# Two scatter accumulators and full 128-row indirect DMAs in a mixture-of-experts kernel

## The reference

```python
def moe_ffn(x, router_w, router_bias, w_gate, w_up, w_down, sw_gate, sw_up, sw_down):
    ...
    _, idx = lax.top_k(scores + router_bias.astype(jnp.float32), TOP_K)
    ...
    padded = (counts + MOE_ROWS - 1) // MOE_ROWS * MOE_ROWS
    ...
    def expert_block(args):
        tok, e = args
        xb = xt[tok]
        h = jax.nn.silu(xb @ w_gate[e]) * (xb @ w_up[e])
        return h @ w_down[e]

    y = lax.map(expert_block, (row_tok.reshape(n_blocks, MOE_ROWS), blk_exp))
    y = y.reshape(P, D) * row_gate[:, None].astype(x.dtype)
    routed = jax.ops.segment_sum(y, row_tok, num_segments=T)
    shared = (jax.nn.silu(xt @ sw_gate) * (xt @ sw_up)) @ sw_down
    return (routed + shared).reshape(B, S, D)
```

## Time and profile before

| | us |
|---|---|
| median of 3 runs | 2637.62 (2608.13 to 2641.2) |
| the profiled execution | 2625.82 |
| its span, first to last instruction | 2623.9 |

### The profile page before, as it was taken

How to read it: one execution, slowest core, us unless ns; L and a number is a source line. 1 busy time by engine, 2 the same in 40 slices (tenths; PEclk the granted TensorE clock), 3 DMA queues, 4 the chain that set the end, 5 groups by cost and what they waited for, 6 DMA issues and landing times.

```text
span 2623.9 us, 35527 instructions
## 1 busy us (share of the span) xinstructions
PE 2323.8 (89%) x9437; PEld 1630.5 (62%) x9437; DVE 1695.1 (65%) x1753; ACT 1070.3 (41%) x1199; POOL 783.7 (30%) x682
## 2 busy tenths in 40 slices
PE   7652997899999999869999999798999999999995
PEld 4220455666666666647988888554666666666663
DVE  5998455666666667553257788545666666666665
ACT  2334014455555555422233333202455555555552
POOL 3663022444434434320000000002334443444432
PEclk9885989999999999988999999899999999999997
DMA  6110137999999999943232222232899999999995
GB/s 205 42 54 0 35 126 240 334 341 362 356 356 333 332 342 352 318 152 112 89 89 65 81 80 71 85 109 86 284 340 354 358 343 337 327 357 340 337 348 163
DMA packets 189297, 592.57 MB, mean 226 GB/s; under 512 B 18781, under 2 KB 88453, under 8 KB 153908
## 3 DMA queue, kind: packets, MB, share of 16 engines
q1 hardware_dynamic: 165140, 517.92, 54.1%
q0 software_dynamic: 24096, 73.88, 12.0%
HBM read 547.11 MB, written 51.38 MB: 228 GB/s over the span
## 4 chain that ended last, share of the span: by engine, by line
PE 35%; DMA 27%; DVE 12%; POOLq 11%; issue 9%; POOL 4%; ACT 1%; SPq 0%; DVEq 0%; ACTq 0%
DMA acc<-BIG,IDXS 22%; PE PS L1455 10%; POOLq L546 9%; DVE BIG L1084 6%; PE PS L1439 5%; PE PS L1237 4%; DMA BIG<-xrows,IDXG 3%; PE PS L1367 3%; PE PS L1346 3%; PE PS L1271 2%; POOL IDXS L586 2%; DMA W<-in_exp_w_up 2%; POOL IDXG L572 1%; PE PS L1468 1%; PE PS L1493 1%
## 5 line engine op out<-in xcount | busy, mean ns | idle before, releaser
L995 DVE TENSOR_TENSOR WL<-W,WH 128x2048 fp32r<-128x2048 f32 x276 | 627.9, 2291 | 276.6 <-ACT WH L691 276.0
L691 ACT ACTIVATE WH<-W 128x2048 fp32r<-128x2048 f32 x276 | 523.0, 1911 | 127.0 <-DMA W<-in_exp_w_up 118.0
L1367 PE MATMUL PS<-W,BIG 128*128 128x512 f32 x1104 | 510.6, 606 | 2.0 <-DVE BIG L1007 2.0
L1346 PE MATMUL PS<-WH,XH 128*128 128x512 f32 x1104 | 443.5, 402 | 5.8 <-DVE XL L988 5.5
L1346 PE MATMUL PS<-WH,XL 128*128 128x512 f32 x1104 | 432.2, 391 | 0.0
L1346 PE MATMUL PS<-WL,XH 128*128 128x512 f32 x1104 | 430.3, 390 | 0.0
L595 POOL DMA_INDIRECT acc<-BIG,IDXS x138 | 304.1, 2204 | 313.4 <-issue 295.3
L1367 PEld LDWEIGHTS PS<-W,BIG 128*128 128x128 f32 x1104 | 205.1, 196 | 209.3 <-issue 206.7
L1346 PEld LDWEIGHTS PS<-WH,XH 128*128 128x128 f32 x1104 | 208.1, 189 | 48.4 <-issue 8.7
L1346 PEld LDWEIGHTS PS<-WH,XL 128*128 128x128 f32 x1104 | 207.5, 188 | 45.2
L1346 PEld LDWEIGHTS PS<-WL,XH 128*128 128x128 f32 x1104 | 208.3, 189 | 39.2
(11 more groups left out here) (233 smaller groups left out, 3174.4 us busy)
## 6 DMA issues: line engine op xcount, KB each, us to landing
W<-in_exp_w_gate SPq DMA_DIRECT2D x138, 1024.0 KB, 8.1
W<-in_exp_w_up SPq DMA_DIRECT2D x138, 1024.0 KB, 11.3
W<-in_exp_w_down SPq DMA_DIRECT2D x138, 1024.0 KB, 7.0
RAW<-in_w_kv SPq DMA_DIRECT2D x48, 512.0 KB, 3.8
RAW<-in_attn_w_q SPq DMA_DIRECT2D x24, 512.0 KB, 3.7
W<-in_conv_w_in SPq DMA_DIRECT2D x8, 1024.0 KB, 11.4
acc<-BIG SPq DMA_DIRECT2D x9, 512.0 KB, 3.7
W<-in_conv_w_out SPq DMA_DIRECT2D x4, 1024.0 KB, 6.6
```

The costliest lines, as they stand in the source:

```text
L691: A(WH[:, s, c, :], W[:, 3 * s + c, :], ACT.Copy).then_inc(s_wh[l], 1)
L995: v.tensor_tensor(WL[s][:, c, :], W[:, 3 * s + c, :], WH[:, s, c, :].bitcast(F32), ALU.subtract).then_inc(s_wl[l], 1)
L1346: last = mm(PS[:, 3 + s, :].rearrange("p (a b) -> p a b", a=2), a, w, start=(k == 0 and i == 0), stop=(k == KT - 1 and i == 2))
L1367: last = mm(PS[:, 5 + h, :], HTm[:, s, k * P:(k + 1) * P], wd[:, k, h * 512:(h + 1) * 512], start=(k == 0), stop=(k == 1))
```

## The change

- `acc` loses its 128 spare rows, and each layer gets a second table of 512 rows, `acc_odd[l]`, which is set to zero at the start from a cleared tile (2 MB each).
- Blocks with an even number scatter to `acc`, those with an odd one to `acc_odd[l]`. `scatter(b)` waits for scatter `b - 2` alone; each slot has a semaphore of its own. `out_low` and `out_high` wait for the same event as before, named by the new semaphores.
- `some_slots` and `by_size` are gone. Each gather and scatter names all 128 rows, with a bounds check of T - 1 in both.
- After the loop SyncE loads both tables, 8 transfers of 512 KB instead of 4, and VectorE adds the two tiles ahead of the statistics (4 additions a layer).
- The semaphores of the routing tables (`s_pj`, `s_tb`) are one for both layers.

```diff
-                def some_slots(b):
-
-                    return [pool.value_load(IDX[i:i + 1, bass.ds(b, 1)].bitcast(I32), min_val=0, max_val=T + P)
-                            for i in (48, 64, 80, 96)]
-
-                def by_size(slots, rows):
...
                 def gather(b, s):
 
-                    slots = some_slots(b)
                     pool.tensor_copy(IDXG[:, s:s + 1], IDX[:, bass.ds(b, 1)]).then_inc(s_ic[l], 1)
                     pool.wait_ge(s_ic[l], b + 1 if isinstance(b, int) and b < 3 else b * 2 - 2)
                     pool.sem_inc(s_go, 1)
...
-                    by_size(slots, rows)
...
+                    pool.indirect_dma_start(XG[:, s, :], None, xrows, bass.IndirectOffsetOnAxis(IDXG[:, s:s + 1], axis=0),
+                                            bounds_check=T - 1, oob_is_err=False).then_inc(s_ga[l][s], 16)
+
+                def scatter(b, s, it, copies):
+
+                    if not (isinstance(b, int) and b < 2):
+                        pool.wait_ge(s_scat[l][s], it * 16)
+                        pool.sem_inc(s_go, 1)
                     pool.tensor_copy(IDXS[:, s:s + 1], IDX[:, bass.ds(b, 1)]).then_inc(s_ic[l], 1)
                     pool.wait_ge(s_ic[l], copies)
                     pool.wait_ge(s_ya[l], b + 1)
                     pool.wait_ge(s_yv[l], b + 1)
-                    if not (isinstance(b, int) and b == 0):
-                        pool.wait_ge(s_scat[l], b * 16)
                     pool.sem_inc(s_go, 1)
...
+                    pool.indirect_dma_start((acc, acc_odd[l])[s], bass.IndirectOffsetOnAxis(IDXS[:, s:s + 1], axis=0),
+                                            YB[:, s, :], None, bounds_check=T - 1, oob_is_err=False,
+                                            compute_op=ALU.add).then_inc(s_scat[l][s], 16)
...
+                sp.wait_ge(s_scat[l][0], n * 16)
+                sp.wait_ge(s_scat[l][1], n * 16)
                 for t in range(NT):
-                    if t == 0:
-                        sp.wait_ge(s_scat[l], n * 32)
                     sp.dma_start(X[:, t, :], acc[t * P:(t + 1) * P, :]).then_inc(s_xin[t], 16)
+                    sp.dma_start(XO[:, t, :], acc_odd[l][t * P:(t + 1) * P, :]).then_inc(s_xin[t], 16)
...
-            sp.dma_start(acc[T:T + P, :], XG[:, 0, :]).then_inc(s_zero, 16)
+            for l in range(2):
+                sp.dma_start(acc_odd[l].rearrange("(n p) d -> p n d", p=P),
+                             XG[:, 0:1, :].broadcast_to([P, NT, D])).then_inc(s_zero, 16)
...
-                        dve.wait_ge(s_xin[n], 16 * (r // 2 + 2))
+                        dve.wait_ge(s_xin[n], 16 + 32 * (r // 2 + 1))
+                        link(v.tensor_tensor(X[:, n, :], X[:, n, :], XO[:, n, :], ALU.add))
```

More of the change, by code:

```diff
@@ L47, in build @@
     xrows = nc.dram_tensor("xrows", [T, D], F32, kind="Internal").ap()
-    acc = nc.dram_tensor("acc", [T + P, D], F32, kind="Internal").ap()
+    acc = nc.dram_tensor("acc", [T, D], F32, kind="Internal").ap()
+    acc_odd = [nc.dram_tensor(f"acc_odd{i}", [T, D], F32, kind="Internal").ap() for i in range(2)]
     etab = nc.dram_tensor("etab", [2, OVER], I32, kind="Internal").ap()
@@ L181, in build @@
         XG = big(13568, 2, D)
+        XO = big(13568, NT, D)
         YB = big(17664, 2, D)
@@ L216, in build @@
         s_ob = sem("overflow_bases")
-        s_pj = [sem(f"onehots{i}") for i in range(2)]
-        s_tb = [sem(f"table_steps{i}") for i in range(2)]
+        s_pj = sem("onehots")
+        s_tb = sem("table_steps")
         s_tab = sem("tables_ready")
@@ L245, in build @@
         s_yv = [sem(f"expert_out_high_copied{i}") for i in range(2)]
-        s_scat = [sem(f"scattered{i}") for i in range(2)]
+        s_scat = [[sem(f"scattered{i}_{k}") for k in range(2)] for i in range(2)]
         s_ph, s_pl = sem("piece_high"), sem("piece_low")
@@ L574, in gather @@
                     pool.sem_inc(s_go, 1)
-                    def rows(r):
-                        pool.indirect_dma_start(XG[0:r, s, :], None, xrows,
-                                                bass.IndirectOffsetOnAxis(IDXG[0:r, s:s + 1], axis=0),
-                                                bounds_check=T - 1, oob_is_err=False).then_inc(s_ga[l][s], 16)
-                    by_size(slots, rows)
-                def scatter(b, s, copies):
-                    slots = some_slots(b)
+                    pool.indirect_dma_start(XG[:, s, :], None, xrows, bass.IndirectOffsetOnAxis(IDXG[:, s:s + 1], axis=0),
[4 more added lines that the diff above has]
+                        pool.sem_inc(s_go, 1)
                     pool.tensor_copy(IDXS[:, s:s + 1], IDX[:, bass.ds(b, 1)]).then_inc(s_ic[l], 1)
@@ L605, in moe, with step @@
                     pool.wait_ge(s_acc[l][k], 16 * NT // 2)
-                def step(b, s):
+                def step(b, s, it):
                     pool.wait_ge(s_tx[l], b + 2)
                     gather(b + 3, 1 - s)
-                    scatter(b, s, b * 2 + 5)
-                step(0, 0)
-                step(1, 1)
+                    scatter(b, s, it, b * 2 + 5)
+                step(0, 0, 0)
+                step(1, 1, 0)
                 with pool.Fori(1, n - 2) as it:
-                    step(it * 2, 0)
-                    step(it * 2 + 1, 1)
-                step(n * 2 - 4, 0)
-                for k in range(3):
-                    scatter(n * 2 - 3 + k, (1 + k) % 2, n * 4 - 2 + k)
+                    step(it * 2, 0, it)
+                    step(it * 2 + 1, 1, it)
+                step(n * 2 - 4, 0, n - 2)
+                scatter(n * 2 - 3, 1, n - 2, n * 4 - 2)
+                scatter(n * 2 - 2, 0, n - 1, n * 4 - 1)
+                scatter(n * 2 - 1, 1, n - 1, n * 4)
             def mix_in(l, n):
@@ L1319, in moe @@
                                   start=(n == 0 and j == 0), stop=(n == NT - 1 and j == 7))
-                    last.then_inc(s_tb[l], 1)
+                    last.then_inc(s_tb, 1)
                 sh_down(2)
```

63 lines of the change are left out of this document (21 added, 42 removed).

## The result

| | before | after |
|---|---|---|
| median | 2632.92 us (2608.13 to 2641.2) | 2706.14 us (2704.09 to 2707.84) |
| span of the profiled execution | 2623.9 us | 2704.8 us |
| loops, first to last output copy, layer 0 and 1 | 718 and 732 us | 752 and 772 us |

The ratio is 1.0285, with a 95% interval of 1.0235 to 1.0336: slower, by 73 us of median and 81 us of span. 74 of these 81 us lie in the two loops; the rest is at their ends. The forecast was 2795 us, so the sign was right and the size about half.

A forecast was written before the change was run, and what follows sets the result against it. The prediction took the DMA engines to be within a few per cent of the bound, with TensorE close. It summed 2625.8 + 156 (loops) + 10 (additions) = 2792 us, put the median at 2795, range 2660 to 2890 us.

The forecast's parts named there:

- What bounds the kernel now: Expert block loops: DMA engines within a few per cent of the bound; late gathers stretch TensorE's 10.0 us to 10.8.
- Part 1: Second accumulator and removed branches: gathers start earlier, worth at most 0.8 us a block, nothing where DMA becomes slower.
- Part 2: 128 named rows in gathers and scatters: real rows load half the engines, 12.0 us a block for 10.8.
- Rows, 4.2 us: Most loaded DMA engine, each block: 8 gathered and 8 scattered rows at 0.27 us each, over 1.02.
- Weights, 8.15 us: DMA engines' time for a block's weights, even over all 16: 8.3 us, over 1.02.
- The lower bound: Block pace with quickest rows: weights 7.65 us at 411 GB/s plus 16 rows at 0.24 us, over 1.02: 11.2 us.
- Steps counted: Loops of both layers: 130 of 138 blocks take the slower pace, 130 x (12.0 - 10.8) = +156 us.
- Part 3: Ends of the layers: four added VectorE tiles a layer, +10 us; reads about +1 us a layer; zero stores at most 2.
- Hidden anyway: Rival for the loops: row at 0.2 us, weights 7.65, pace 10.7 to 11.0 us, 2623 to 2662 us; chance 0.12.
- Spread evenly: Rival on row placement: engines share rows evenly, pace 10.0 to 10.2 us, 2532 to 2558 us; chance 0.13.
- TensorE's clock: Rival for the loops: steady waits lower the clock, TensorE's 10 us grow to 13 or more, 2948 us; chance 0.10.
- What would show it: Signs in the profile after: copies 11.2 to 12.4 us apart, TensorE 80 to 88% busy, DMA some 80%, up-matrix waits doubled.

The follow-up runs named there:

- before_early: Kernel before with only GpSimd's order changed, gather b + 4 issued ahead of scatter b: 2597.6 us, ratio 0.9857, 10.59 us a block.
- one_acc_plain: Kernel after with one accumulator and the old wait for scatter b - 1, 128 rows named in plain order: 2694.6 us, ratio 1.0236.
- the four placements: Kernel after and three copies with only the slots of rows permuted; 4.2, 6.4, 7.1, 7.8 rows on the busiest engine: 10.19, 10.95, 11.41, 11.79 us a block.
- plain_5mb: Kernel after with one of three gate and up terms, gate and up matrices loaded twice, no low parts: 3320.3 us, 16.05 us a block.
- norows_5mb: plain_5mb with every row index out of bounds, so all rows are named and none moved: 2877.1 us, 12.65 us a block.
- norows_short_early: norows_short_pe with gather b + 4 issued ahead of scatter b: 2299.2 us, ratio 0.8738, 8.25 us a block.
- two_acc_spread: Kernel after with the rows of a block dealt out over all 16 DMA engines by permuted slots: 2554.0 us, ratio 0.9701.
- plain_short_pe: Kernel after with one of the three terms of the gate and up products: 2690.3 us, ratio 1.0215, 11.38 us a block.
- the packed kernel: Kernel after with slots permuted so that one DMA engine is filled with eight rows before the next: 2755.3 us, ratio 1.0467.
- norows_short_pe: plain_short_pe with every row index out of bounds, so all rows are named and none moved: 2518.0 us, ratio 0.9555, 10.05 us a block.

## Why the prediction was right in kind and wrong in size

The direction and the mechanism were right: slower, because the rows of a block sit on half of the engines. The size was not: +1.2 us a block was forecast and +0.60 measured, +162 us in all against +73. The stated range of 2660 to 2890 us holds the measured 2706 because it is wide, not because the sum was right.

- **What bounds the kernel now** held. DMA was within a few per cent of being the bound: a DMA share of 1.00 at 10.59 us a block (before_early) shows where it lay, 0.2 us under the 10.81 of the kernel before.
- **Part 1** held. "Worth nothing where DMA becomes the slower one" is what one_acc_plain shows: equal pace, other wait. Gathers were late, but a shorter turn and an earlier landing are only two cures of it. The gather also stands behind a scatter that waits for an output copy; that wait the prediction did not name, and moving the gather ahead of it is a third.
- **Part 2**, the spreading of rows and its sign, held, by the four placements. The step that failed is the sum: "I take 12.0, somewhat nearer the upper end, because the loop's own mean price is the nearest row". Measured were 11.41 us, near the lower end. The sum at the upper end is 8.15 us for weights (8.3 over 1.02) and 4.2 us for rows (16 x 0.27 over 1.02), 12.4 in all.
  - *Rows, 4.2 us:* too large by 0.8 us. plain_5mb over norows_5mb gives 3.40. Of this, some 0.3 us are the count, eight on the busiest engine where the blocks of these inputs have 7.4; the prediction named blocks of few rows and gave them no number. The rest is the price, 0.46 us a pair for 0.53.
  - *Weights, 8.15 us:* too large by 0.56 us if norows_5mb's 7.59 holds, which agrees with the 7.65 at 411 GB/s that the prediction kept for its lower bound. But no run shows 7.59 in a loop with the normal 3.146 MB: norows_short_early took 8.25.
  - *The parts measured apart do not give the whole.* 7.59 + 3.40 = 10.99 us, 0.42 under the measured 11.41; 8.25 + 3.40 = 11.65, 0.24 over. The row term is the one that is shown to be mis-sized; how much of the remaining error is the weights' stays open.
  - *The lower bound* was added wrongly as well: 11.5 over 1.02 is 11.3, not 11.2, and 411 GB/s are bytes by time that passed, not by busy time of engines, so the division by 1.02 does not apply to the 7.65. Without it the bound is 7.65 + 3.8 / 1.02 = 11.4. That is what was measured, but with the 3.40 of rows that plain_5mb shows it is not, so the agreement may be luck.
- **Steps counted.** 130 x (11.41 - 10.81) = 78 us, and the loops grew by 74. Forecast were 156, and nearly all of the excess is the pace; the count of 130 was close.
- **Part 3** held: 10 us for additions and a little for reads were forecast, 11.5 us measured. No cost of the zero stores was seen.
- **Hidden anyway** came nearest among the rivals. Its 7.65 us for weights agree with norows_5mb, its 3.1 us for rows (16 x 0.2 over 1.02) are 0.3 under the measured 3.40, and the two terms measured apart make its upper edge of 11.0 us. The loop ran 0.4 us above that edge. **Spread evenly** is what two_acc_spread does on purpose: forecast for it were 2532 to 2558 us, measured 2554. **TensorE's clock** did not fall in the kernel after (1.00 and 0.99 with 9% of idle time); at 28% of idle time, in plain_short_pe, it was granted at 0.86, and even so the time did not rise.
- **What would show it.** Right: distance of copies, q0's packets, GpSimd idle over half the time (262.68 of 650 us busy), no wait for a scatter, small gather waits. Wrong: TensorE at 91%, not 80 to 88, which follows from 11.4 in place of 12.0 (0.91 x 11.41 / 12.0 = 0.87), and DMA at 91%, not some 80, which follows only in part (0.87 by the same scaling). ScalarE's waits for the up matrix did not double but went from 54.1 to 47.4 us; those for all weights grew from 55 to 239 us, by the gate matrix. Once the queue is behind all the time, the first of the two to be waited for is the late one; this is argued from the order of the queue and not shown by a run. That the chain of the page leads through the up matrix (22% of the span) fits it.

One point stays open. With the normal 3.146 MB and no rows (norows_short_early) a block took 8.25 us, not 7.59. Its DMA share was 0.99, not 1.02, and TensorE, VectorE and ScalarE each had short waits, so other floors (VectorE has 7 us of work a block) may have held it. And norows_5mb reads two of its matrices twice, which may make their bytes cheaper than in a normal loop. What speaks for the forecast's price is q1's share of the 16 engines: 73.5% of 11.41 = 8.4 us a block in the kernel after (460 to 1110 us), as the 8.3 of the kernel before, where norows_5mb has 7.6 for the same bytes. No run settles why.

## What to carry to other kernels

A transfer that names 128 partitions and skips the empty ones is not spread over the DMA engines by what it moves, but by the slots that it names: if the real rows come first and fill about half of the slots, half of the engines do the row work, and the loads beside it land late. Deal the rows out over the slots; here it was worth 152 us, twice what the change cost. And where a wait goes away and the pace stays, look for the wait that took its place: in the kernel after it was the gate matrix, in the kernels with little TensorE work a ring through GpSimd's queue, found in order of time.

## What was not expected of the hardware

- A mean DMA share of 0.91, or 0.88, does not tell that DMA has room: in the packed kernel at 0.88 the loop ran at 11.79 us, and the same bytes took 10.19 us evenly spread.
- The first index copy behind an indirect DMA on GpSimd takes 0.75 to 2.23 us in the trace (the rows of norows_short_pe and of after above); copies of the kernel before took 0.18 and 0.80 us. What it waits for the rows do not show.
- With no row to move, a gather still took 8.5 us from its issue at 904.82 us to the transposes that waited for it at 913.28, 2.24 us of them for the issue, with a DMA share of 0.82.
- 16 engines carried 414 GB/s in the mean over 650 us (norows_5mb), as in the best 5 us of the kernel before.
